# Deferring block products of a Strassen MLP, its differences kept in PSUM, and a later wait for weight sums

## What is computed

```python
def _sq_relu_mlp(h, w1, w2):
    return jnp.square(jax.nn.relu(h @ w1)) @ w2
...
        h_lat = h_lat + g2 * _sq_relu_mlp(_modulate(_rms_norm(h_lat, norm2_g[i]), sh2, sc2), mlp_w1[i], mlp_w2[i])
```

## Time and profile before

| what | value |
|---|---|
| median of 3 runs | 2434.31 us (2430.83 to 2434.5) |
| the profiled execution | 2434.44 us, span 2432.9 us, mean granted clock 0.976 |
| PE busy | 2263.9 us (93%), 11430 matmuls |
| weight loads of PE | 1871.9 us (77%) |
| DVE busy | 1782.4 us (73%) |
| ACT busy | 1158.8 us (48%) |
| POOL busy | 1193.0 us (49%) |

### The profile page before, as it was taken

The page is one execution under the profiler, slowest core; times in us unless marked ns, Lnnn a source line. Parts: engine busy times, 40 slices in busy tenths (PEclk is TensorE's granted clock), DMA queues, the critical chain, the costliest instruction groups (busy, mean ns, idle before and its releaser), DMA issues. The chain is left out here.

```text
span 2432.9 us, 38281 instructions
## 1 busy us (share of the span) xinstructions
PE 2263.9 (93%) x11430; PEld 1871.9 (77%) x11430; DVE 1782.4 (73%) x2843; ACT 1158.8 (48%) x2133; POOL 1193.0 (49%) x970
## 2 busy tenths in 40 slices
PE   5989979999999999999699799888998999999998
PEld 3768868888888888888587677776776777777777
DVE  5653787777777777777674688881688888888887
ACT  5553443333333333333443588883345554545454
POOL 0003623433333444333646577665636767767674
PEclk9999999999999999999789899999999999999999
DMA  7434213444443345444412211105111212121222
GB/s 269 176 131 175 66 52 104 120 130 116 116 129 103 110 116 137 112 120 120 135 44 104 93 29 40 31 27 190 54 38 49 78 56 74 60 73 57 73 61 83
DMA packets 106153, 234.27 MB, mean 96 GB/s; under 512 B 9424, under 2 KB 18000, under 8 KB 102736
## 3 DMA queue, kind: packets, MB, share of 16 engines
q1 hardware_dynamic: 94432, 209.57, 26.1%
q0 software_dynamic: 8704, 16.78, 4.2%
q10 hardware_dynamic: 2928, 6.82, 0.8%
HBM read 216.35 MB, written 50.33 MB: 110 GB/s over the span
## 5 line engine op out<-in xcount | busy, mean ns | idle before, releaser
L877 POOL TENSOR_TENSOR ht<-ht,l_side 128x512 f32<-128x512 f32 x112 | 150.5, 1344 | 507.4 <-ACT l_side L1004 503.3
L51 PE MATMUL l_z_ps<-nh,l_w1h 128*128 128x512 f32 (+1 forms) x816 | 292.9, 359 | 6.6 <-POOL l_w1l L58 3.4
L53 PE MATMUL l_z_ps<-nh,l_w1l 128*128 128x512 f32 (+1 forms) x816 | 291.7, 358 | 0.0
L52 PE MATMUL l_z_ps<-nl,l_w1h 128*128 128x512 f32 (+1 forms) x800 | 285.7, 357 | 0.0
L1308 DVE SCALAR_TENSOR_TENSOR ht<-l_yy_ps,mod,ht 128x512 f32<-128x512 f32 x336 | 233.9, 744 | 10.9 <-PE l_yy_ps L1624 10.0
L2791 PE MATMUL l_yy_ps<-l_ah,l_w2h 128*128 128x512 f32 x448 | 182.3, 407 | 26.6 <-DVE ht L2582 25.7
L2083 POOL TENSOR_TENSOR ht<-ht,l_side 128x512 f32<-128x512 f32 x112 | 154.2, 1377 | 107.5 <-ACT l_side L2258 106.9
L58 POOL TENSOR_TENSOR l_w2l<-l_w2f,l_w2h 128x512 fp32r<-128x512 f32 x128 | 180.1, 1412 | 33.9 <-ACT l_w2h L2213 30.2
L3520 POOL TENSOR_TENSOR sc<-sc,den 128x640 f32<-128x640 f32 (+1 forms) x128 | 149.5, 1200 | 91.9 <-DVE den L3602 91.9
L58 POOL TENSOR_TENSOR l_w1l<-early,l_w1h 128x512 fp32r<-128x512 f32 x104 | 148.7, 1431 | 77.0 <-ACT l_w1h L2203 77.0
L1622 PE MATMUL l_yy_ps<-l_ah,l_w2h 128*128 128x512 f32 x448 | 178.4, 398 | 6.1 <-DVE ht L1308 6.1
(11 more groups left out here) (339 smaller groups left out, 6486.5 us busy)
## 6 DMA issues: line engine op xcount, KB each, us to landing
l_aw<-ada SPq DMA_DIRECT2D x128, 256.0 KB, 3.0
maw<-ada SPq DMA_DIRECT2D x24, 1024.0 KB, 5.1
l_w1f<-w SPq DMA_DIRECT2D x32, 512.0 KB, 3.8
l_w2f<-w SPq DMA_DIRECT2D x32, 512.0 KB, 4.2
sums<-w SPq DMA_DIRECT2D x32, 512.0 KB, 5.1
sums<-w POOLq DMA_DIRECT2D x32, 512.0 KB, 7.9
early<-w SPq DMA_DIRECT2D x50, 256.0 KB, 2.6
l_w2f<-w SPq DMA_DIRECT2D x48, 256.0 KB, 2.6
```

What stands on the lines that cost most here:

```text
L51: pe.matmul(out, lh, rh, start=first, stop=False)
L52: pe.matmul(out, lh, rl, start=False, stop=False)
L53: return pe.matmul(out, ll, rh, start=False, stop=last)
```

## The change

It has four parts, all but the first in `strassen_tail`.

1. POOL's wait for the sums at the end of layer 0's MLP goes. SP waits for them in the tail, ahead of the first loads of W2 blocks.
2. Six of the seven products of a pair are deferred (`DEFERRED` is now a table): product 1 stands behind the next pair's M1, 2 behind M5, 3 behind M6, 4 behind M2, 5 behind M7, 6 behind M3; product 0 alone follows M4.
3. The second pair defers as well. It runs its four blocks in a row, then product 0, and its products 1 to 6 stand between the hidden products of pair 2. The token sums' rounding and low parts are moved to fit, with the four low parts of T1, T3 and T4 inside DVE's `pair(PLAIN, True)`.
4. The differences are formed in another order, T3, T2, T1 and T4, and T2, T1 and T4 lie in PSUM, T1 in B11's place and T4 in T2's; T3 lies in a slot of SBUF. The orders of operands and their buffers (`A_ORDER`, `A_BUF`, `A_AFTER`) follow, as do the waits that protect them.

The orders of ACT, DVE, POOL and SP change with it. The core of the diff:

```diff
@@ layer 0's MLP, POOL
                 outputs(PAIRS - 1, False)
-                if C:
-                    pool.wait_ge(s_sums, 32 * PAIRS)
@@ strassen_tail
-    DEFERRED = 2
+    DEFERRED = {"M1": 1, "M5": 2, "M6": 3, "M2": 4, "M7": 5, "M3": 6}
...
-    A_ORDER = ["B11", "T2", "T3", "T4", "B21", "T1", "B22"]
-    A_BUF = {"B11": 0, "B21": 0, "T2": 1, "B22": 1, "T3": 2, "T4": 3, "T1": 4}
-    A_AFTER = {"B11": (1, 6), "B21": (0, 0), "T2": (1, 5), "B22": (0, 1), "T1": (1, 4)}
+    A_ORDER = ["B11", "T2", "T3", "T4", "T1", "B21", "B22"]
+    A_BUF = {"B11": 0, "B22": 0, "T2": 1, "B21": 1, "T3": 2, "T4": 3, "T1": 4}
+    A_AFTER = {"B11": (1, 5), "B22": (0, 0), "T2": (1, 6), "B21": (0, 1), "T1": (1, 4)}
...
-    T_AT = {"T1": 1, "T2": 2, "T3": 3, "T4": 4}
-    HOME_BANK = {"B11": 1, "T4": 1, "T3": 2, "B22": 3}
-    HOME_SLOT = {"T1": 0, "B12": 1, "B21": 2, "T2": 3}
+    T_AT = {"T3": 1, "T2": 2, "T1": 3, "T4": 4}
+    HOME_BANK = {"B11": 1, "T1": 1, "T2": 2, "T4": 2, "B22": 3}
+    HOME_SLOT = {"B12": 1, "B21": 2, "T3": 3}
@@ SP
+                sp.wait_ge(s_sums, 32 * PAIRS)
                 for i in (0, 4, 2, 3):
                     load2(0, i)
@@ DVE, diff(p, name)
+                    if name == "T3":
+                        after_square(dve, p, "B22")
                         after_square(dve, p, "B12")
-                        after_square(dve, p, "B22")
-                        dve.wait_ge(s_al, operand_at(p, "B11"))
-                        dve.tensor_tensor(inner("T1"), inner("B11"), inner("B12"), ALU.subtract).then_inc(s_t, 1)
+                        dve.tensor_tensor(inner("T3"), inner("B22"), inner("B12"), ALU.subtract).then_inc(s_t, 1)
                     elif name == "T2":
-                        dve.wait_ge(s_t, t_at(p, "T1"))
-                        after_square(dve, p, "B22")
-                        dve.scalar_tensor_tensor(out=inner("T2"), in0=inner("T1"), scalar=-1.0, in1=inner("B22"), op0=ALU.mult, op1=ALU.subtract).then_inc(s_t, 1)
+                        dve.wait_ge(s_t, t_at(p, "T3"))
+                        dve.wait_ge(s_al, operand_at(p, "B11"))
+                        dve.scalar_tensor_tensor(out=inner("T2"), in0=inner("B11"), scalar=-1.0, in1=inner("T3"), op0=ALU.mult, op1=ALU.subtract).then_inc(s_t, 1)
@@ PE
-                def pair(p, earlier=True):
-                    behind = {"M1": 2, "M5": 3, "M6": 4, "M2": 5, "M3": 6}
+                def pair(p):
                     for prod in Z_ORDER:
                         hidden(p, prod)
-                        if earlier and prod in behind:
-                            product(p - 1, behind[prod])
-                    for i in range(DEFERRED):
-                        product(p, i)
+                        if prod in DEFERRED:
+                            product(p - 1, DEFERRED[prod])
+                    product(p, 0)
...
-                for name in ("B11", "B12", "B22"):
+                for name in ("B11", "B12", "B22", "B21"):
                     plain_block(1, (name,))
                 product(1, 0)
-                plain_block(1, ("B21",))
-                for i in range(1, 7):
-                    product(1, i)
-                pair(PLAIN, False)
-                with pe.Fori(PLAIN + 1, PAIRS - 1) as p:
+                pair(PLAIN)
+                with pe.Fori(PLAIN + 1, PAIRS) as p:
                     pair(p)
-                pair(PAIRS - 1)
-                for i in (2, 3):
+                for i in (1, 2, 3):
                     product(PAIRS - 1, i)
```

More of the change, by code:

```diff
@@ L2160, in _ @@
                     add(0, i)
-                for j in range(HK):
-                    low_t("T2", j)
                 low2(1, 1)
@@ L2168, in _ @@
                 low2(1, 2)
+                for j in range(HK):
+                    low_t("T2", j)
                 add(1, 0)
@@ L2433, in _ @@
                 pair(last, False)
+                side_read(last, 1)
+                high2(last, 4)
+                high(last, "B21")
+                high(last, "B22")
                 side_read(last, 2)
@@ L2692, in _ @@
                 square(0, "B22")
-                plain_rest(0)
+                diffs(0)
+                low(0, "T2")
+                low(0, "T3")
+                acc(0, 0, (0, 1))
+                diff(0, "T4")
+                acc(0, 0, (2, 3))
+                low(0, "T4")
+                low(0, "T1")
+                acc(0, 1)
+                low(0, "B21")
+                low(0, "B22")
+                acc(0, 2)
+                low2(0, 6)
+                sum2(0, 5)
+                acc(0, 3)
+                low2(0, 5)
+                acc(0, 4)
+                acc(0, 5)
+                acc(0, 6)
                 low2(1, 0)
@@ L2702, in _ @@
                 square(1, "B12")
+                for j in range(HK):
+                    second_sum(j)
                 square(1, "B22")
-                plain_rest(1)
-                pair(PLAIN, False)
+                diffs(1)
+                low(1, "T2")
+                for j in range(HK):
+                    fourth_sum(j)
+                low(1, "T3")
+                acc(1, 0, (0, 1))
+                diff(1, "T4")
+                acc(1, 0, (2, 3))
+                pair(PLAIN, True)
                 with dve.Fori(PLAIN + 1, PAIRS) as p:
                     pair(p)
-                pair_start(PAIRS)
-                acc(PAIRS - 1, 5)
-                acc(PAIRS - 1, 6)
+                last = PAIRS - 1
+                low(last, "T4")
+                low(last, "T1")
+                acc(last, 1)
+                low(last, "B21")
+                low(last, "B22")
+                acc(last, 2)
+                low2(last, 6)
+                sum2(last, 5)
+                acc(last, 3)
+                low2(last, 5)
+                for i in (4, 5, 6):
+                    acc(last, i)
                 for i in range(len(HALVES)):
```

212 lines of the change are left out of this document (76 added, 136 removed).

## The result

| | before | after |
|---|---|---|
| median | 2433.91 us (20 runs, 2429.95 to 2436.01) | 2439.55 us (20 runs, 2435.65 to 2441.91) |
| ratio | 1 | 1.0024, 95% interval 1.0017 to 1.0031 |
| span of the profiled execution | 2432.9 us | 2439.4 us |
| PE busy | 2263.9 us | 2262.4 us |
| DVE busy | 1782.4 us | 1763.2 us |

The change costs 5.6 us, where 8.1 of gain were forecast. The measured time lies above the forecast's range. DVE and POOL do less work than before, PE the same; the span grew all the same. Among the 20 runs of the changed kernel those at a mean granted clock of 0.975 lie from 2439.9 to 2441.8 us and those at 0.978 from 2436.2 to 2439.0, so a difference of some 3 us between two medians is hardly clear of this spread.

A forecast was written before the change was run, and what follows sets the result against it. PE was taken to bound the loop, so only its waits count. Layer 0's end −4.4, second pair −9.5, loop +5.8 and end 0 sum to −8.1 from 2434.44: 2426.3 us, own range 2419 to 2433, wider range 2412 to 2436.

The forecast's parts named there:

- the walk: Loop: item-by-item count from the end of product 5 to M1's weights, putting M1 1.46 us late, 1.58 with slow restart.
- 12 times +5.8: Loop: M1's stall of 1.58 us per pair replaces a lost 1.1, +0.48 each, +5.8 us over 12 pairs.
- A: Loop: M1's weights come in time, no stall, the loop gains 13.2 us, 2407 us; 11 in 100.
- B: Loop: B21's relu goes first, only 0.72 us lost per pair in place of 1.1, 2416 us; 13 in 100.
- C: Loop: DVE and POOL block each other on M1's path, 1.5 to 1.6 us more per pair, 2445 us; 7 in 100.
- The second pair: Second pair and first Strassen pair: 15.1 us of present losses go, 5.6 of new ones come, −9.5 us.
- (a): Second pair: M1 of pair 2 waits for the relu of B21, behind DVE's sums and ACT's T4 rounding; 0.7 us lost.
- (b): Second pair: M5 of pair 2 waits for T1's low parts, ready at 1837.3, due at 1835.9; 1.6 us lost.
- the three places I had named: Second pair: M1 of pair 2, M5, and M1 of pair 3, forecast at 0.7, 1.6 and 3.3 us.
- Rival D: Second pair: its new stalls are followed by half clock, −2 us in place of −9.5, 2433.8 us; 9 in 100.
- The end of layer 0: Layer 0's end: without the wait POOL is done when its issue ends, next block starts at 1189.0; −4.4 us.
- The end: Behind the last pair: the 2.28 us stall should split into smaller ones; between −4 and +2, about 0.

The follow-up runs named there:

- the experiment on ACT's order: Changed kernel with the rounding (split) of the next M1's weights moved ahead of T2's rounding on ACT: 2415.3 us, ratio 0.9926.
- Four orders: Kernel with split ahead of T2, second pair reordered, last sums issued earlier, and three further second-pair orders of it: 2411.08, 2409.9, 2412.25, 2411.64 us.
- the other order: Second pair with T1's parts and B21's relu earlier, here with split ahead of T2 and earlier transfer, against the changed kernel: 2411.08 us, ratio 0.9903.

## Why the prediction was wrong

Point by point, by its own steps.

- **The loop: the walk was right, its term somewhat small.** The stall is where it was forecast, M1 1.54 us late for 1.46, the period 40.28 for 40.2. Every link of the walk is within 0.1 us of the rows, and the experiment on ACT's order took the whole stall away. "12 times +5.8" measured +8.3: the period gives +7.0 (0.58 for 0.48), and 1.4 more are M1 of pair 3, which after its 2.67 us of waiting ran at a granted clock of 0.63. Rivals A and B are out. So is C: POOL lengthened no link of the walk but the one that it had priced so (DVE's low part of W2, 1.36).
- **The second pair: this step failed, 9.6 of the 14.5 us.** The step was (a), "the third and the first sum from 1813.41 (2.73 for four pieces)", with POOL's items said to be "nothing" but for M6. I took these durations of DVE from a stretch in which POOL had stood idle, and the same change puts POOL's five items right into it. What it measured: 3.79 and 6.29 for the third and the second sum. Two more terms failed beside it: the fourth sums took 4.76 for the 2.74 before, and in (b) "the four pieces at 0.6", T1's low parts, took 5.87 in place of 2.4, which is the whole of the wait before M5. Where the forecast lost 5.6 us, the trace lost 5.63, 3.09 and 2.67 in the three places I had named, together 11.4, and 3.0 more because the blocks behind the first two took 4.30 and 4.27 us in place of 2.77; some restarts make the rest. The contended row was in my hands (1.37 for a low part of 0.68), and I priced it in the loop only, where it did not matter. The bound "If the pieces run beside POOL and cost twice, or half clock follows a stall, −7" took one of the two; both came. The slow block behind M1's wait is not a loss of its own: M5 is released by DVE's low parts 10.3 us after M1's start whether M1's block is short or long. With the split ahead of T2, where M1's block ran longer (its twelve matmuls took 5.24 us), the wait before M5 was 2.16 in place of 3.09. Rival D said −2 for this stretch and had the slow matmuls right, as a cause of its own; it is the nearest of my cases here, and did not name the contention.
- **The end of layer 0: this step failed, 3.9 us.** "Without it POOL is done when its issue ends" is false here. The block's end waits for POOL's own transfer, wait or no wait; −0.2 in the gap, where −4.4 was forecast.
- **The end**: −1.5 inside the −4 to +2 given. The stall of 2.28 us became five of 0.2 to 0.7, and the granted clock of the stretch went from 0.97 to 1.00.
- **The sum.** Two gains that were not there, 13.5 us, and 2.5 more in the loop, 1.5 less at the end: 14.5, which is 6.4 − (−8.1).

What the change was made for, six deferred products, does pay once M1's weights are in time: a pair then takes 38.65 us, 1.05 less than the 39.70 before, about 13 us in all. It was given back in ACT's order, because the deferral halved the time between M4 and the next M1, left the split of M1's weights behind T2, which had become later, and put it behind the square of B21 as well. The square alone is 0.66 us a pair of this, by the experiment that moved the split past it. How much of the rest is the new order of the differences and how much the place of B11's low part, no run separates.

What stays open: whether the second pair's 7 to 9 us of waiting can go at all. Four orders moved it without lessening it. DVE is close to full there: in the changed kernel it is busy 31.8 of the 32.6 us from 1812.9 to 1845.5, part of that being what POOL adds to its instructions. ACT (19.5) and POOL (22.6) are not full, and with the other order POOL stands idle for 10.29 us in a row. No run took work away from DVE or put POOL's five items into that gap, so whether a fifth order would do better is not shown.

## What to carry to other kernels

When work is moved, ask for each engine what runs beside it in the new place: a duration from a trace holds only with the neighbours that it had. After deferring or tightening a schedule, look for the instruction whose window got shorter (same buffer, less time between its last reader and its next use) and move it to where its inputs are ready; half a microsecond in the queue of an engine that is half idle cost this kernel 8 us. A wait that is taken off a block's end gains nothing while the same engine's transfer is still on its way; issue the transfer earlier instead.

## What the runs showed that I had not expected

- The end of a block waits for the landing of a transfer that POOL issued, without a wait in the program: 5.89 us of gap with one on its way, 1.75 without.
- DVE and POOL beside each other both lose: two POOL splits took 4.92 us for 2.6, and the four sums beside them and the two items behind 6.29 for 2.74. T1's low parts took 2.49 with POOL idle and 5.87 beside it.
- The matmuls behind a wait are not always slow. Behind the wait of 2.67 us before M1 of pair 3 the first one took 0.79 and the block of twelve 4.31; behind 2.01 in the same place, with the split one instruction up, 0.50. Behind a wait of 2.90 us in pair 0 it took 0.50 in the kernel with the split ahead of T2 and 0.80 in the one with POOL's items narrowed.
